# Attention of a hybrid decoder step: exponentials in the score banks, one normalising product, and separate buffers for one weight unit

## The reference

```python
def _sink_probs(s, mask, sink):
    s = jnp.where(mask, s, NEG_INF)
    m = jnp.maximum(jnp.max(s, axis=-1, keepdims=True), sink)
    p = jnp.exp(s - m)
    return p / (jnp.sum(p, axis=-1, keepdims=True) + jnp.exp(sink - m))
...
    o = jnp.einsum('bnhgqk,bnkhd->bnqhgd', p, v_band).reshape(B, L, ATTN_WIDTH)
...
    mixed = jnp.concatenate([_pool_mix(u, pos_p, pool_w[l], pool_scale[l]),
                             _swa_prompt(q, k, v, attn_sinks[l])], axis=-1)
    xp = xp + mixed @ w_out[l]
```

## Time and profile before

| | us |
|---|---|
| median of 3 runs | 889.54 (889.29 to 892.64) |
| profiled execution | 889.57 |
| its span, first to last instruction | 887.8 |
| TensorE busy | 876.8 (99%) |
| VectorE busy | 663.6 (75%) |
| ScalarE busy | 397.0 (45%) |
| GpSimd busy | 32.6 (4%) |

### The profile page before, as it was taken

The page is one execution under the profiler, slowest core; times in us unless marked ns, Lnnn a source line. Parts: engine busy times, 40 slices in busy tenths (PEclk is TensorE's granted clock), DMA queues, the critical chain, the costliest instruction groups (busy, mean ns, idle before and its releaser), DMA issues.

```text
span 887.8 us, 17081 instructions
## 1 busy us (share of the span) xinstructions
PE 876.8 (99%) x7104; PEld 859.7 (97%) x7104; DVE 663.6 (75%) x957; ACT 397.0 (45%) x639; POOL 32.6 (4%) x37
## 2 busy tenths in 40 slices
PE   9999999999999999999999999999999999999998
PEld 8999999999999999999777999999999999999998
DVE  7969556997579986745787587997469985799844
ACT  8635213554125543444754356554125542255520
POOL 0000000000000000013322000000000000000000
PEclk9999999999999999999999999999999999999999
DMA  7333313432433323512401413423323424244231
GB/s 261 104 121 129 131 48 119 134 105 85 142 119 118 122 84 94 182 51 81 129 24 31 162 49 121 150 87 126 124 95 133 131 84 143 91 135 131 84 120 61
DMA packets 43180, 98.57 MB, mean 111 GB/s; under 512 B 4288, under 2 KB 5056, under 8 KB 43104
## 3 DMA queue, kind: packets, MB, share of 16 engines
q1 hardware_dynamic: 41376, 95.01, 32.3%
q10 hardware_dynamic: 1728, 2.48, 0.8%
HBM read 93.53 MB, written 3.60 MB: 109 GB/s over the span
## 4 chain that ended last, share of the span: by engine, by line
PE 93%; DVE 4%; ACT 1%; issue 1%; DMA 1%; SPq 0%; DVEq 0%; ACTq 0%
PE ps L608 43%; PE ps L737 15%; PE ps L739 15%; PE ps L738 15%; PE ps L639 1%; DVE prob L1916 1%; PE ps L796 1%; DMA raw<-gu 1%; DVE wlo L1520 1%; PE ps L962 0%; PE ps L980 0%; ACT prob L1381 0%; PE ps L880 0%; DVE small L1900 0%; PE ps L654 0%
## 5 line engine op out<-in xcount | busy, mean ns | idle before, releaser
L737 PE MATMUL ps<-xhi,whi 128*128 128x260 f32 (+1 forms) x1092 | 310.2, 284 | 0.1
L739 PE MATMUL ps<-xhi,wlo 128*128 128x260 f32 (+1 forms) x1092 | 310.0, 284 | 0.0
L738 PE MATMUL ps<-xlo,whi 128*128 128x260 f32 (+1 forms) x1092 | 309.5, 283 | 0.0
L737 PEld LDWEIGHTS ps<-xhi,whi 128*128 128x128 f32 x1092 | 205.3, 188 | 0.8 <-issue 0.6
L739 PEld LDWEIGHTS ps<-xhi,wlo 128*128 128x128 f32 x1092 | 205.5, 188 | 0.0
L738 PEld LDWEIGHTS ps<-xlo,whi 128*128 128x128 f32 x1092 | 205.4, 188 | 0.0
L1591 DVE TENSOR_TENSOR wlo<-full,whi 128x1024 fp32r<-128x1024 f32 (+1 forms) x117 | 160.3, 1394 | 0.0
L1116 ACT CAST whi<-raw 128x1024 fp32r<-128x1024 f32 (+1 forms) x75 | 75.2, 1003 | 165.2 <-PE ps L608 158.2
L608 PE MATMUL ps<-hhi,whi 128*128 128x268 f32 (+1 forms) x690 | 140.4, 285 | 0.3
L608 PE MATMUL ps<-hlo,whi 128*128 128x268 f32 (+1 forms) x690 | 140.1, 284 | 0.0
L608 PE MATMUL ps<-hhi,wlo 128*128 128x268 f32 (+1 forms) x690 | 139.7, 284 | 0.0
(11 more groups left out here) (198 smaller groups left out, 1086.4 us busy)
## 6 DMA issues: line engine op xcount, KB each, us to landing
full<-gu SPq DMA_DIRECT2D x78, 512.0 KB, 4.3
raw<-d SPq DMA_DIRECT2D x32, 448.0 KB, 3.4
full<-gu SPq DMA_DIRECT2D x39, 256.0 KB, 2.7
raw<-d SPq DMA_DIRECT2D x16, 512.0 KB, 3.9
raw<-w_in SPq DMA_DIRECT2D x10, 512.0 KB, 3.7
raw<-gu SPq DMA_DIRECT2D x9, 512.0 KB, 4.0
raw<-w_out SPq DMA_DIRECT2D x8, 512.0 KB, 3.8
xT<-x SPq DMA_DIRECT2D x8, 268.0 KB, 5.6
```

The source lines that it names most:

```text
L737: nc.tensor.matmul(dst, whi_t, xhi_t, start=(first and pr == 0), stop=False, skip_group_check=True)
L738: nc.tensor.matmul(dst, whi_t, xlo_t, start=False, stop=False, skip_group_check=True)
L739: last = nc.tensor.matmul(dst, wlo_t, xhi_t, start=False, stop=(pr == KC - 1), skip_group_check=True)
```

## The change

Three things change.

- `exps` writes the exponentials over the scores in PSUM rather than to `prob`, and no longer waits for the transposes of step i - 2. `normalise` makes one product of all four heads, from PSUM times the reciprocals (a column per head, repeated along it) into `prob`; ahead of it VectorE waits for the transposes of step i - 2.
- Output unit 2 gets buffers of its own, `whi3` and `wlo3`, where `zg`, `zsq` and `partner` lay. So its split no longer waits for unit 0, but for the three semaphores that say that those tiles are used up, and it is moved ahead of the output units on both engines.
- At the end of attention, VectorE makes the last pooled mean first and then the output residual of step 7 and the split of unit 1.

```diff
+    whi3, o = place("whi3", [P, KD, P], F32R, offset=xhi_end)
+    wlo3, o = place("wlo3", [P, KD, P], F32R, offset=o)
...
+    def whi_of(c):
+        return whi3 if c == U_OUT + 2 else whi[:, c % 2, :, :]
...
             act.wait_ge(raw_loaded[c % RAW], 16 * (c // RAW + 1))
-            if c >= 2:
+            if c == U_OUT + 2:
+                act.wait_ge(sin_ready, 5)
+                act.wait_ge(rot_ready, 5)
+                act.wait_ge(nsum_filled, 5)
+            elif c >= 2:
                 act.wait_ge(unit_done, c - 1)
-            nc.scalar.copy(whi[:, c % 2, 0:t, :], raw[:, c % RAW, 0:t, :]).then_inc(whi_ready, 1)
+            nc.scalar.copy(whi_of(c)[:, 0:t, :], raw[:, c % RAW, 0:t, :]).then_inc(whi_ready, 1)
...
         def exps(i):
             act.wait_ge(nmax_ready, i + 1)
-            if i >= 2:
-                act.wait_ge(probs_turned, i - 1)
             s = i % 2
             for j in range(GQ):
-                nc.scalar.activation(prob[:, s, j, :], banks_of[i % 3][:, j // 2, (j % 2) * 2 * P:(j % 2 + 1) * 2 * P],
-                                     ACT.Exp, scale=qscale(i, j), bias=small[:, s, 4 + j:5 + j],
+                sc = banks_of[i % 3][:, j // 2, (j % 2) * 2 * P:(j % 2 + 1) * 2 * P]
+                nc.scalar.activation(sc, sc, ACT.Exp, scale=qscale(i, j), bias=small[:, s, 4 + j:5 + j],
                                      accum_out=small[:, s, 12 + j:13 + j])
...
             chain(nc.vector.reciprocal(small[:, s, 24:28], small[:, s, 20:24]))
-            for j in range(GQ):
-                last = nc.vector.tensor_scalar(prob[:, s, j, :], prob[:, s, j, :], small[:, s, 24 + j:25 + j], None,
-                                               ALU.mult)
-            last.then_inc(prob_ready, 1)
+            if i >= 2:
+                dve.wait_ge(probs_turned, i - 1)
+            inverse = small[:, s, 24:28].rearrange("p (j o) -> p j o", o=1).to_broadcast([P, GQ, 2 * P])
+            nc.vector.tensor_tensor(prob[:, s, :, :], banks_of[i % 3].rearrange("p s (j k) -> p (s j) k", k=2 * P),
+                                    inverse, ALU.mult).then_inc(prob_ready, 1)
...
         pool_out(2)
+        pool_mean(3)
+        out_lo(7)
         split_next(9)
-        out_lo(7)
-        pool_mean(3)
+        split_lo(U_OUT + 2)
         pool_out(3)
```

More of the change, by code:

```diff
@@ L234, in build @@
     assert o <= xlo_at
+    whi3, o = place("whi3", [P, KD, P], F32R, offset=xhi_end)
+    wlo3, o = place("wlo3", [P, KD, P], F32R, offset=o)
+    assert o <= xlo_at
     qT, o = place("qT", [P, GQ, NOUT], offset=xlo_end)
@@ L417, in build, with wlo_of @@
               dict(s=1, ua=U_A2, ub=U_B2, ea=E_A2, eb=E_B2, c0=META, n=NH_OUT)]
+    def whi_of(c):
+        return whi3 if c == U_OUT + 2 else whi[:, c % 2, :, :]
+    def wlo_of(c):
+        return wlo3 if c == U_OUT + 2 else wlo[:, c % 2, :, :]
     def blocks(n):
@@ L605, in product @@
                     wait_k(k)
-                for w, lo in ((whi, 0), (whi, 1), (wlo, 0)):
+                for i, (w, lo) in enumerate(((whi_of(c), 0), (whi_of(c), 1), (wlo_of(c), 0))):
                     for h in range(2):
-                        last = nc.tensor.matmul(dst[:, h, 0:n], w[:, c % 2, kk, :], x(k, lo, h),
-                                                start=(k == begin and w is whi and not lo),
-                                                stop=(k == end and w is wlo))
+                        last = nc.tensor.matmul(dst[:, h, 0:n], w[:, kk, :], x(k, lo, h),
+                                                start=(k == begin and i == 0), stop=(k == end and i == 2))
             if not ks or ks[-1] == end:
@@ L1472, in _ @@
         pool_hi(2)
+        split_hi(U_OUT + 2)
         pool_hi(3)
         for d in range(KD):
-            split_hi(U_OUT + d + 2)
+            if d:
+                split_hi(U_OUT + d + 2)
             act.wait_ge(evacuated, E_OUT + d + 1)
@@ L1519, in split_lo @@
             dve.wait_ge(whi_ready, c + 1)
-            nc.vector.tensor_tensor(wlo[:, c % 2, 0:t, :], raw[:, c % RAW, 0:t, :],
-                                    whi[:, c % 2, 0:t, :].bitcast(F32), ALU.subtract).then_inc(wlo_ready, 1)
+            nc.vector.tensor_tensor(wlo_of(c)[:, 0:t, :], raw[:, c % RAW, 0:t, :],
+                                    whi_of(c)[:, 0:t, :].bitcast(F32), ALU.subtract).then_inc(wlo_ready, 1)
         def x_lo(lo, hi, t, d, g, c0, n):
@@ L2050, in _ @@
             nc.vector.tensor_tensor(x_d, outpair[d % 2][:, :, 0:NH_OUT], x_d, ALU.add).then_inc(evacuated, 1)
-            split_lo(U_OUT + d + 2)
+            if d:
+                split_lo(U_OUT + d + 2)
             x_lo(x_pair(xlo7, d, NH_OUT), x_pair(xhi7, d, NH_OUT), d, d, 2, META, NH_OUT)
```

## The result

| | before | after |
|---|---|---|
| median of 6 runs, us | 889.78 (887.82 to 892.86) | 883.04 (882.74 to 885.01) |
| profiled execution, us | 889.57 | 883.07 |
| its span, us | 887.8 | 881.0 |
| TensorE busy, us | 876.8 | 874.0 |
| VectorE busy, us | 663.6 | 657.6 |

The ratio is 0.9921, 95% interval 0.9899 to 0.9943; measured again beside the last experiments it was 0.9938 (0.9924 to 0.9951). The forecast was 882.2 us in a range of 881.0 to 884.7: the time lies inside.

The account below looks back on a forecast made before the run. TensorE was taken as the bound, with room only in its waits from attention to the third output unit. Gains 3.36 + 0.78 + 1.70 + 1.49 = 7.33 us took 889.57 to 882.2 us, range 881.0 to 884.7.

Parts of the forecast that it names:

- Part 1: Attention steps: in-place exponentials and one 1.22 us PSUM product replacing four scalings, not held up by GpSimd; gain 3.36 us.
- The four waits: TensorE waits in attention of 1.17, 0.71, 0.24 and 0.60 us, to go; 3.36 us with what the brackets hide.
- the tight one: TensorE's 0.60 us wait at 475.55 in step 6; a reduction 0.8 us earlier just covers 0.60 + 0.16.
- a doubling: Counter-case for the PSUM product: 1.14 us doubled to 2.28, leaving 0.4 us of step 6's saving; time about 882.9.
- In-place exponentials: ScalarE's 32 passes, now written to PSUM, taken at 0.56 us each; 0.77 if reading and writing one bank alternate.
- Part 2: End of attention: last pooled mean moved ahead of a split and a residual; TensorE's 0.62 us wait goes, gain 0.78 us.
- Part 3: Output unit 2 with own buffers, splits moved earlier: 1.99 us lost ahead of it shrinks to about 0.3, gain 1.7.
- The clock: Unit 2 at full granted clock, gain 1.49 us; rival that the clock still falls: 883.7 us, chance 0.11.
- the pause of 1.84 us: TensorE's wait before the third output unit, longest in the stretch; the granted clock was 0.50 after it.
- small operations: Rival: GpSimd delays the maxima's three small operations in every step, waits at 458.80 and 475.55 stay; 883.4 us, chance 0.08.
- fall behind in the output units: Rival: VectorE lags in the output units and up to 3.2 us returns; 884 to 885.5 us, chance 0.07.
- In-place passes: Slower rival: in-place exponential passes cost far more; at 1.25 us each the gain is used up; chance 0.03.

Follow-up runs that it names:

- unit 2 in free banks: Changed kernel with output unit 2 written to the score steps' PSUM banks, free by then, instead of the pair unit 0's evacuation empties; median 884.01 us, ratio 0.9922.

## Why the prediction was right, and where it was not

- **What bounds the kernel.** Right: all of the gain lies in the waits of the earlier trace rows and the clock behind them. Matmul for matmul, the two traces keep their distance everywhere else behind the start-up to 0.1 us.
- **Part 1.** The product took 1.22 us in all eight steps, as taken, and was not held up. The four waits gave 3.13 us of the 3.36 foretold; each term was met within 0.1 us, the tight one with 0.67 of 0.76. Half wrong was the reason in the step that led there: I put the gain on the PSUM source, and with an SBUF source the time was the same. The rule of the Trainium skill, VectorE: DVE Perf Modes, section Mode 2×_2P, which I had weighed as a doubling, shows in part: four scalings from PSUM take 1.66 us where four within SBUF take 1.14, 1.46 times as long, while the one product takes 1.22.
- **In-place exponentials.** 0.533 us, below the 0.56 taken. The Trainium skill, ScalarE: Activation LUTs, section Step-by-step: what each stage is for, has a tip that ScalarE writes PSUM faster than SBUF; 533 against 561 ns agrees. It moved nothing.
- **Part 2.** 0.79 of 0.78 us.
- **Part 3.** 1.74 of 1.70 us; 0.25 us is left where 0.3 was said, and it is the evacuation, as said.
- **The clock.** The term came out, 1.47 us between the two traces for 1.49, and one fall less by the medians. The step that stood behind it failed: the fall was put down to the pause of 1.84 us because it followed it in the one trace at hand. Four traces with that pause have none behind it, and four have one at 428 us, with no wait of TensorE ahead of it. The term is a draw in each execution, none to three falls of 1.4 to 1.7 us, and the profile of before happened to have one and the profile of after none. That it was met is luck: unit 2 in free banks, which does less waiting still, had a fall in 4 of 6 runs and a median of 884.01.
- **What was not foreseen.** The wait of 0.38 us ahead of the third pool map, which the changed instruction count brings. With it the sum without the clock is 3.13 + 0.79 + 1.74 - 0.35 = 5.3 us, beside 5.2 between the runs without a fall. The 0.8 us by which the time lies above the forecast is this wait, 0.23 that part 1 gave less, and 0.3 outside the span: the profiled execution is 2.1 us longer than its span, where 1.8 was taken.
- **The other rivals.** GpSimd still holds up small operations of step 3, the first and the third (0.64 and 1.16 us for four columns, against 0.16 or 0.17 in steps 4 to 7), but TensorE did not wait for them. VectorE did not fall behind in the output units, and TensorE has no wait there. In-place passes did not cost more.

```profile
435.03 0.64 DVE L1914 TENSOR_TENSOR small<-small,qnrm 128x4 f32<-128x4 f32 x1
435.71 0.16 DVE L1916 SCALAR_TENSOR_TENSOR small<-small,nsink 128x4 f32<-128x4 f32 x1
435.90 1.16 DVE L1919 TENSOR_TENSOR small<-small,fixed 128x4 f32<-128x4 f32 x1
```

## What to carry to other kernels

Where VectorE works beside GpSimd, look at the form of its instructions, not at its busy time: four scalings within SBUF were held up one after another, one product of the same data at most once. A fall of the clock seen in one trace is a draw: count it over many executions before it enters a sum as a certain term or gets a cause. And after an edit that changes the number of instructions, look for a wait at a place that the edit did not touch.

## What was not expected of the hardware

- The granted clock fell to 0.50 between 428 and 432 us with no idle time on TensorE ahead of it, after 1.95 us of two-column matmuls. The Trainium skill, TensorE: Matmul & The Clock Gate, Part 1, section What's actually happening, lists the lower clock for an idle TensorE; the rows show no idle time there, and the fall came in some executions only.
- A product with two SBUF inputs and GpSimd's adds hold each other up: 0.76 us on VectorE and 0.87 on GpSimd for one meeting.
- The place in VectorE's instruction stream is worth 0.35 us, the same in five traces.
